# Both score matmuls of an attention kernel contract over all 128 partitions: each key band holds one part, high or low, on both halves of the partitions

## The chip, the cores and the metric

The kernel runs on one core of one Trainium2 chip. The metric is the device time of one execution in microseconds (us), from the first to the last instruction of the core, as the median of repeated runs.

## The reference

One layer of a streaming encoder: a normalised input is projected by one large weight matrix, a pooling mixer and a windowed attention run side by side, both are gated, and an output projection is added to the input. Cut to what matters here:

```python
def _gqa_sink_attend(q, k, v, mask, sinks):
    s = jnp.einsum('bcqhgd,bckhd->bchgqk', q, k) * (HEAD_DIM ** -0.5)
    s = jnp.where(mask[None, :, None, None, None, :], s, NEG_INF)
    sink = jnp.broadcast_to(sinks[None, None, :, :, None, None], s.shape[:-1] + (1,))
    p = jax.nn.softmax(jnp.concatenate([s, sink], axis=-1), axis=-1)[..., :-1]
    return jnp.einsum('bchgqk,bckhd->bcqhgd', p, v)

def reference(x, ...):            # h = [16 meta tokens; 1024 frames], D_MODEL = 2048
    hn = _rmsnorm(h, norm_g)
    proj = hn @ w_in
    pv, pg, q, k, v, ag = jnp.split(proj, SPLITS, axis=-1)
    pool_out = _multiscale_pool(pv, pool_w, pool_scale)
    attn_out = _attention_branch(q, k, v, q_norm_g, k_norm_g, sinks)
    mixed = jnp.concatenate([silu(pg) * pool_out, silu(ag) * attn_out], axis=-1)
    h = h + mixed @ w_out
```

There are 16 query heads and 2 key heads of dimension 64. The frames are cut into chunks of 64. The queries of a chunk see the 16 meta tokens, the previous chunk and their own chunk: 16 + 64 + 64 = 144 keys.

## The kernel before

**Precision.** Every matrix product is made of parts. A float32 number is split into a high part (rounded to the narrow matmul type, fp32r, by a copy on ScalarE, ACT) and a low part (the float32 number minus the high part, by a subtraction on VectorE, DVE). A projection is three matmuls: weight high by activation high, weight high by activation low, weight low by activation high (lines 1058, 1059 and 1062).

**Tiling and staging.** The 1024 frames are handled in two halves of 512 (`h` = 0, 1). In each half TensorE (PE) first projects keys and values (8 weight blocks of 128x512), then the 8 pairs of query heads (32 blocks), then 4 groups (`g`) of 24 blocks each, and then the output projection. Weight blocks come by DMA into `raw` (4 slots), ACT makes `wh`, DVE makes `wl`. ACT and DVE prepare the block three steps ahead of the one that TensorE works on, and ACT waits for a slot until TensorE has finished the block that was in it (`s_blk`).

**Key bands.** While the queries are projected, `k_band` on ACT (step 18) and on DVE (step 21) lays out the keys: for each key head `e` a band with 9 pieces of 64 + 16 columns, the 64 keys of a chunk and the 16 meta keys. `band_h` and `band_x` are both 128 partitions high. Before, `band_h` holds the high part on partitions 0 to 63 (its other half is not used), and `band_x` holds the low part on partitions 0 to 63 and the high part on 64 to 127. ACT counts its copies on `s_kbh`, DVE's last subtraction counts on `s_kbl`.

**Attention inside the groups.** A group has four units (`u` = 0 to 3), each of four chunks and two heads. A unit is worked between the blocks of the group: the scores after block 4u+3, the transposes of the probabilities after block 4u+8, the product with the values after block 4u+10. The order is written out by hand on each engine (`when` on TensorE, `todo` on ACT and DVE). The stationary operand of the scores, `qs[:, c]`, holds the high part of the queries on partitions 0 to 63 and the low part on 64 to 127. Per chunk there are two score matmuls of 144 columns into the PSUM tile `S`: line 1180 takes 64 partitions (query high by key high), line 1181 takes all 128 (query high by key low, plus query low by key high). In the first half the first chunk gets a third matmul that adds the mask, line 1184, which runs as two passes.

Four units by four groups by two halves are 32 units, with 8 score matmuls each: 256 in all. Eight of the 32 units have the mask.

**Around the scores on DVE.** `row_max` (line 890, output `smax`) waits for the last score matmul of the unit (`s_s`). `silu` (its reciprocal is line 948) follows in the same step of the list for `u` = 0 and 1. `p_low` (outputs `pt` and `pm`) waits for ACT's copies of the transposed probabilities, and the values matmuls (lines 1206 and 1210) wait for `p_low`.

**Around the bands on DVE.** After `k_band` come the low part of a weight block, `q_norm` (a reciprocal, line 842, and a product, line 844), another weight block and `square_low` (output named `d_l`, whose memory it uses), for which the sum of squares on TensorE (lines 1145 and 1146) waits.

Of the kernel before, what the change touches and what calls it, by code (L numbers as in the profile page):

```python
# [16 lines left out]
P = 128  # L17
D = 2048
KT = D // P
META = 16  # L20
# [9 lines left out]
CHUNK = 64  # L30
NCH = HALF // CHUNK
HD = 64
# [4 lines left out]
BAND = META + CHUNK  # L37
# [41 lines left out]
def hymba_layer(nc, xcat, norm_g, w_in, w_out, pool_w, vecs, consts, out):  # L79
# [6 lines left out]
    with ctx:  # L86
        def sb(name, shape, dt=f32):
            return ctx.enter_context(nc.sbuf_tensor(name, shape, dt))
# [11 lines left out]
        kT = sb("kT", [P, CHUNK + HALF])  # L100
        vT = sb("vT", [P, CHUNK + HALF])
        k_meta = sb("k_meta", [P, META])
# [13 lines left out]
        band_h = sb("band_h", [P, KVH, (NCH + 1) * BAND], f32r)  # L116
        band_x = sb("band_x", [P, KVH, (NCH + 1) * BAND], f32r)
# [310 lines left out]
        def _(act):  # L428
            def copy(dst, src):
                return nc.scalar.activation(dst, src, ACT.Copy)  # L430
# [55 lines left out]
            for h in range(HALVES):  # L486
# [36 lines left out]
                def k_band():  # L523
                    act.wait_ge(s_kn, SPANS_BY[h + 1])
                    for e in range(KVH):
                        src = slice(e * HD, (e + 1) * HD)
                        for band, dst in ((band_h, slice(0, HD)), (band_x, slice(HD, P))):
                            kb = band[dst, e, :].rearrange("p (c n) -> p c n", n=BAND)
                            copy(kb[:, :, 0:CHUNK],
                                 kT[src, :].rearrange("p (c n) -> p c n", n=CHUNK)).then_inc(s_kbh, 1)  # L530
                            copy(kb[:, :, CHUNK:BAND],
                                 k_meta[src, :].unsqueeze(1).to_broadcast([HD, NCH + 1, META])).then_inc(s_kbh, 1)
# [21 lines left out]
                for s in range(Q_BLKS + 1):  # L554
                    if s and s % 4 == 0:
                        q_square(s // 4 - 1)
                    if s < Q_BLKS:
                        split_high(h4 + KV_BLKS // RAW, s + LEAD)
                    if s > 4 and s % 4 == 1:
                        q_sqrt(s // 4 - 1)  # L560
                    if s == 2:
                        v_all_out()
                    if s == 18:
                        k_band()
                    if s == 23:
                        v_operand(0)
# [156 lines left out]
        def _(dve):  # L723
            def sub(dst, a, b):
                return nc.vector.tensor_tensor(dst, a, b, ALU.subtract)  # L725
# [63 lines left out]
            for h in range(HALVES):  # L789
# [26 lines left out]
                def k_band():  # L816
                    for e in range(KVH):
                        src = slice(e * HD, (e + 1) * HD)

                        high = (band_h, band_x)[e][src, e, :].rearrange("p (c n) -> p c n", n=BAND)  # L820
                        low = band_x[0:HD, e, :].rearrange("p (c n) -> p c n", n=BAND)
                        dve.wait_ge(s_kbh, 8 * h + (2, 8)[e])
                        sub(low[:, :, 0:CHUNK], kT[src, :].rearrange("p (c n) -> p c n", n=CHUNK),
                            high[:, :, 0:CHUNK])
                        ins = sub(low[:, :, CHUNK:BAND],
                                  k_meta[src, :].unsqueeze(1).to_broadcast([HD, NCH + 1, META]),
                                  high[:, :, CHUNK:BAND])
                    ins.then_inc(s_kbl, 1)

                def v_operand(e):  # L830
# [16 lines left out]
                for s in range(Q_BLKS + 1):  # L847
                    if s and s % 4 == 0:
                        square_low(s // 4 - 1)
                    if s < Q_BLKS:  # L850
                        split_low(h4 + KV_BLKS // RAW, s + LEAD)
                    if s > 4 and s % 4 == 2:
                        q_norm(s // 4 - 1)
                    if s == 21:
                        k_band()
                    if s == 25:
                        v_operand(0)
# [186 lines left out]
        def _(pe):  # L1044
            mm = nc.tensor.matmul
# [61 lines left out]
            for h in range(HALVES):  # L1107
# [58 lines left out]
                def group(g, e, late):  # L1166
                    G = h * GROUPS + g

                    def scores(u):
                        pe.wait_ge(s_qdl, G * UNITS + u + 1)  # L1170
                        pe.wait_ge(s_ex, ONE + (G * UNITS + u) * (QUAD + 1))
                        pe.wait_ge(s_kbh, 8 * (h + 1))
                        pe.wait_ge(s_kbl, ONE + h + 1)
                        for c in range(QUAD):
                            ch = (u % 2) * QUAD + c
                            o = S[:, c // 2, (c % 2) * KEYS:(c % 2 + 1) * KEYS]
                            at = slice(ch * BAND, ch * BAND + KEYS)
                            q = qs[:, c, :, :].rearrange("p a t -> p (a t)")
                            masked = h == 0 and ch == 0
                            mm(o, q[0:HD], band_h[0:HD, e, at], start=True, stop=False)  # L1180
                            last = mm(o, q, band_x[:, e, at], start=False, stop=not masked)  # L1181
                            if masked:

                                last = mm(o, ident, cst[:, C_MASK:C_MASK + KEYS],
                                          start=False, stop=True)
                        last.then_inc(s_s, 1)
# [29 lines left out]
                    for u in range(UNITS):  # L1216
                        when.setdefault(4 * u + 3, []).append((scores, u))
                        when.setdefault(4 * u + 8, []).append((transposes, u))
                        when.setdefault(4 * u + 10, []).append((values, u))
# [142 lines left out]
```

## Time and profile before

| | |
|---|---|
| median of 3 runs | 1302.7 us (1301.02, 1302.71, 1302.70) |
| span of the profiled execution | 1300.8 us |
| own time of the profiled execution | not recorded apart from its span |
| TensorE matmul busy | 1279.3 us, 98% |
| weight load busy | 1057.4 us, 81% |
| DVE busy | 895.0 us, 69% |
| ACT busy | 634.8 us, 49% |
| DMA | 103 GB/s over the span |
| granted TensorE clock | full in all 40 slices |

The busy time of TensorE counts matmuls whose ends are modelled and overlap the next one; how fast it gets on is read from the distances between the starts. The weight load (PEld) is listed apart from the matmul (PE) that uses it. A wait shown for an engine is the time that it stood idle before an instruction and who released it.

### The profile page before, as it was taken

The numbers are of one execution on the slowest core, as the hardware profiler recorded it, in microseconds if no ns is written. First come the engines' busy times: TensorE is split into PE (matmuls) and PEld (weight loads), VectorE is DVE, ScalarE is ACT, GpSimd is POOL, SyncE is SP. The second block draws the span as 40 slices with busy tenths as digits, with TensorE's granted clock in tenths as the row PEclk, the third lists the DMA queues.
The fourth block names the chain that finished last, engine by engine and source line by source line (L and its number), as shares of the span: only waits on it lengthen the run. The fifth ranks groups of instructions, "written<-read, shape, count | busy, mean of one in ns | idle before, by whom it ended". The sixth has DMA issues, their size and how long they took to land.

```text
span 1300.8 us, 19299 instructions
## 1 busy us (share of the span) xinstructions
PE 1279.3 (98%) x6200; PEld 1057.4 (81%) x6200; DVE 895.0 (69%) x1417; ACT 634.8 (49%) x1490; POOL 66.5 (5%) x78
## 2 busy tenths in 40 slices
PE   4999999999999999999999999999999999999998
PEld 4988798798888987888888887787887877788887
DVE  7466777878868777665644677777787887854553
ACT  6434356365454554545433344554645545444442
POOL 0000000010010110000000000000101103000000
PEclk9999999999999999999999999999999999999999
DMA  5233322322322225544543332223222222244442
GB/s 213 79 92 97 90 72 75 89 68 63 94 81 75 67 73 185 188 133 157 186 127 89 92 98 86 70 73 88 83 72 79 84 81 74 93 141 137 161 140 86
DMA packets 70609, 134.38 MB, mean 103 GB/s; under 512 B 8064, under 2 KB 10240, under 8 KB 69888
## 3 DMA queue, kind: packets, MB, share of 16 engines
q1 hardware_dynamic: 68160, 125.17, 31.4%
q0 software_dynamic: 2384, 8.39, 1.8%
q8 instruction: 35, 0.57, 0.2%
q14 instruction: 30, 0.25, 0.1%
HBM read 125.14 MB, written 8.39 MB: 103 GB/s over the span
## 4 chain that ended last, share of the span: by engine, by line
PE 94%; DVE 3%; DMA 1%; ACT 1%; issue 1%; SPq 0%; ACTq 0%
PE R L1058 18%; PE R L1059 18%; PE R L1062 18%; PE S L1281 4%; PE S L1282 4%; PE S L1280 4%; PE S L1181 3%; PE S L1180 3%; PE OP L1282 2%; PE OP L1280 2%; PE R L1281 2%; PE OP L1281 2%; PE R L1282 2%; PE R L1280 2%; PE OP L1059 1%; PE OP L1062 1%
## 5 line engine op out<-in xcount | busy, mean ns | idle before, releaser
L430 ACT ACTIVATE wh<-raw 128x512 fp32r<-128x512 f32 x400 | 250.3, 631 | 534.7 <-PE R L1062 310.1
L725 DVE TENSOR_TENSOR wl<-raw,wh 128x512 fp32r<-128x512 f32 x400 | 281.7, 708 | 264.7 <-ACT wh L430 263.6
L1058 PE MATMUL R<-act_h,wh 128*128 128x512 f32 (+1 forms) x1168 | 426.0, 370 | 0.0
L1059 PE MATMUL R<-act_l,wh 128*128 128x512 f32 (+1 forms) x1168 | 422.8, 367 | 0.0
L1062 PE MATMUL R<-act_h,wl 128*128 128x512 f32 (+1 forms) x1168 | 403.5, 366 | 0.0
L1058 PEld LDWEIGHTS R<-act_h,wh 128*128 128x128 f32 x1168 | 220.1, 188 | 36.4 <-DVE wl L725 0.8
L1059 PEld LDWEIGHTS R<-act_l,wh 128*128 128x128 f32 x1168 | 220.1, 188 | 34.7
L1062 PEld LDWEIGHTS R<-act_h,wl 128*128 128x128 f32 x1168 | 210.6, 188 | 36.7
L948 DVE RECIPROCAL scr<-scr 128x512 f32<-128x512 f32 x32 | 107.3, 3353 | 1.1
L402 POOL TENSOR_TENSOR scr<-scr 128x527 f32<-128x527 f32 (+3 forms) x40 | 48.7, 1217 | 837.6 <-ACT pv_last L430 378.2
L430 ACT ACTIVATE pm<-OP 16x128 fp32r<-16x128 f32 x256 | 68.1, 266 | 5.4
L842 DVE RECIPROCAL scr<-scr 128x512 f32<-128x512 f32 x16 | 53.5, 3346 | 4.3 <-ACT scr L551 4.3
L725 DVE TENSOR_TENSOR pt<-PT,pt 128x512 fp32r<-128x512 f32 x32 | 22.1, 691 | 46.9 <-ACT pm L430 46.9
L1282 PE MATMUL S<-wh,band_x 128*128 128x512 f32 x128 | 50.7, 396 | 0.0
L1281 PE MATMUL S<-wl,band_h 128*128 128x512 f32 x128 | 50.6, 395 | 0.0
L1280 PE MATMUL S<-wh,band_h 128*128 128x512 f32 x128 | 50.3, 393 | 0.0
L1280 PE MATMUL S<-wh,v_s 128*128 128x512 f32 x128 | 49.9, 390 | 0.0
L1282 PE MATMUL S<-wh,mix_x 128*128 128x512 f32 x128 | 49.9, 390 | 0.0
L1281 PE MATMUL S<-wl,v_s 128*128 128x512 f32 x128 | 49.8, 389 | 0.0
L610 ACT ACTIVATE scr<-S,nmax 128x144 f32<-128x144 f32 x128 | 46.8, 378 | 0.6
L725 DVE TENSOR_TENSOR mix_x<-mixed,v_s 128x512 fp32r<-128x512 f32 x64 | 43.8, 684 | 0.0
L725 DVE TENSOR_TENSOR band_x<-mixed,band_h 128x512 fp32r<-128x512 f32 x64 | 43.7, 683 | 0.0
(210 smaller groups left out, 1844.5 us busy)
## 6 DMA issues: line engine op xcount, KB each, us to landing
raw<-w_in_blocks SPq DMA_DIRECT2D x272, 256.0 KB, 2.6
raw<-w_out_in SPq DMA_DIRECT2D x128, 256.0 KB, 3.0
scr<-xcat SPq DMA_DIRECT2D x32, 256.0 KB, 4.4
mixed<-xcat SPq DMA_DIRECT2D x4, 1024.0 KB, 7.7
res<-xcat SPq DMA_DIRECT2D x16, 256.0 KB, 3.2
out<-scr POOLq DMA_DIRECT2D x14, 256.0 KB, 2.6
out<-res POOLq DMA_DIRECT2D x14, 256.0 KB, 4.2
scr<-pool_w_in SPq DMA_DIRECT2D x8, 256.0 KB, 3.0
```

What stands on the lines that cost most here:

```text
L402: ins = pool.tensor_tensor(dst[:, lo:COLS], src[:, lo:COLS], src[:, lo - step:COLS - step], ALU.add)
L430: return nc.scalar.activation(dst, src, ACT.Copy)
L610: nc.scalar.activation(prob[:, c, :], S[:, c // 2, (c % 2) * KEYS:(c % 2 + 1) * KEYS], ACT.Exp, bias=nmax[:, c:c + 1], accum_out=den[:, c: ...
L725: return nc.vector.tensor_tensor(dst, a, b, ALU.subtract)
L842: nc.vector.reciprocal(q_rs[t % 2], q_rs[t % 2]).then_inc(s_qrs, 1)
L948: nc.vector.reciprocal(gate[n], gate[n]).then_inc(s_gr, 1)
L1058: mm(o, wh[:, b, w], act_h[:, k, c], start=(k == 0), stop=False)
L1059: mm(o, wh[:, b, w], act_l[:, k, c], start=False, stop=False)
L1062: last = mm(o, wl[:, b, w], act_h[:, k, c], start=False, stop=(k == KT - 1))
L1280: mm(YB[r], mh, wh[:, k % SPLIT, :], start=(k == 0), stop=False)
L1281: mm(YB[r], mh, wl[:, k % SPLIT, :], start=False, stop=False)
L1282: last = mm(YB[r], ml, wh[:, k % SPLIT, :], start=False, stop=(k == KT - 1))
```

## The change

The copies on ACT write the high part of the keys to both halves of the partitions of `band_h`, where two of them went to `band_x` before. The subtractions on DVE write the low part to both halves of `band_x`, so that there are eight of them in a half of the frames where there were four. The first score matmul takes all 128 partitions of `qs` and `band_h`: (query high + query low) by key high. The second takes `band_x` as before, and gives (query high + query low) by key low, with a product of the two low parts that was not computed before.

```diff
@@ ACT k_band
-                        for band, dst in ((band_h, slice(0, HD)), (band_x, slice(HD, P))):
+                        for band, dst in ((band_h, slice(0, HD)), (band_h, slice(HD, P))):
@@ DVE k_band
-                        high = (band_h, band_x)[e][src, e, :].rearrange("p (c n) -> p c n", n=BAND)
-                        low = band_x[0:HD, e, :].rearrange("p (c n) -> p c n", n=BAND)
+                        high = band_h[src, e, :].rearrange("p (c n) -> p c n", n=BAND)
                         dve.wait_ge(s_kbh, 8 * h + (2, 8)[e])
-                        sub(low[:, :, 0:CHUNK], kT[src, :].rearrange("p (c n) -> p c n", n=CHUNK),
-                            high[:, :, 0:CHUNK])
-                        ins = sub(low[:, :, CHUNK:BAND],
-                                  k_meta[src, :].unsqueeze(1).to_broadcast([HD, NCH + 1, META]),
-                                  high[:, :, CHUNK:BAND])
+                        for dst in (slice(0, HD), slice(HD, P)):
+                            low = band_x[dst, e, :].rearrange("p (c n) -> p c n", n=BAND)
+                            sub(low[:, :, 0:CHUNK], kT[src, :].rearrange("p (c n) -> p c n", n=CHUNK),
+                                high[:, :, 0:CHUNK])
+                            ins = sub(low[:, :, CHUNK:BAND],
+                                      k_meta[src, :].unsqueeze(1).to_broadcast([HD, NCH + 1, META]),
+                                      high[:, :, CHUNK:BAND])
                     ins.then_inc(s_kbl, 1)
@@ PE scores
-                            mm(o, q[0:HD], band_h[0:HD, e, at], start=True, stop=False)
+                            mm(o, q, band_h[:, e, at], start=True, stop=False)
                             last = mm(o, q, band_x[:, e, at], start=False, stop=not masked)
```

On DVE, at step 21 of the query projection of the first half, the kernel before has these instructions between two weight blocks and in front of the next query normalisation:

```order
L725 TENSOR_TENSOR band_x<-kT,band_h 64x9x64
L725 TENSOR_TENSOR band_x<-k_meta,band_h 64x9x16
L725 TENSOR_TENSOR band_x<-kT,band_x 64x9x64
L725 TENSOR_TENSOR band_x<-k_meta,band_x 64x9x16
L725 TENSOR_TENSOR wl<-raw,wh 128x512
```

After the change the same place on DVE reads:

```order
L725 TENSOR_TENSOR band_x<-kT,band_h 64x9x64
L725 TENSOR_TENSOR band_x<-k_meta,band_h 64x9x16
L725 TENSOR_TENSOR band_x<-kT,band_h 64x9x64
L725 TENSOR_TENSOR band_x<-k_meta,band_h 64x9x16
L725 TENSOR_TENSOR band_x<-kT,band_h 64x9x64
L725 TENSOR_TENSOR band_x<-k_meta,band_h 64x9x16
L725 TENSOR_TENSOR band_x<-kT,band_h 64x9x64
L725 TENSOR_TENSOR band_x<-k_meta,band_h 64x9x16
L725 TENSOR_TENSOR wl<-raw,wh 128x512
```

Two pairs of subtractions more stand ahead of the weight block `wl`; the same happens in the second half. On ACT and on TensorE the number and the order of the instructions stay; only the operands differ.

## Rows read from the trace of the kernel before

**Rows 1.** Part 1 of the page: busy time, share, instructions.

```profile
PE 1279.3 (98%) x6200; PEld 1057.4 (81%) x6200; DVE 895.0 (69%) x1417; ACT 634.8 (49%) x1490; POOL 66.5 (5%) x78
```

**Rows 2.** The page's chain that ended last, by engine.

```profile
PE 94%; DVE 3%; DMA 1%; ACT 1%; issue 1%; SPq 0%; ACTq 0%
```

**Rows 3.** Waits of TensorE from 150 to 490 us: total, times, longest.

```profile
PE OP L1280 <- DVE mixed L940: 0.4, 1, 0.4
```

**Rows 4.** Line 1180: duration min/median/max in ns, first and last start.

```profile
L1180 PE MATMUL S<-band_h,qs x128: 329/331/336, 157.4 to 1092.4; 64*128 64x144 f32 x128
```

**Rows 5.** Timeline of TensorE's matmuls, an unmasked unit: start, duration.

```profile
170.44 0.40 PE L1059 MATMUL R<-act_l,wh 128*128 128x512 f32 x1
170.68 0.39 PE L1062 MATMUL R<-act_h,wl 128*128 128x512 f32 x1
171.00 0.33 PE L1180 MATMUL S<-band_h,qs 64*128 64x144 f32 x1
171.26 0.33 PE L1181 MATMUL S<-band_x,qs 128*128 128x144 f32 x1
...
173.01 0.33 PE L1058 MATMUL R<-act_h,wh 128*128 128x264 f32 x1
```

**Rows 6.** Timeline of the weight loads of the same unit.

```profile
170.45 0.19 PEld L1062 LDWEIGHTS R<-act_h,wl 128*128 128x128 f32 x1
171.00 0.18 PEld L1180 LDWEIGHTS S<-band_h,qs 64*128 64x128 f32 x1 [0.36 <-issue]
...
172.84 0.19 PEld L1181 LDWEIGHTS S<-band_x,qs 128*128 128x128 f32 x1
172.94 0.19 PEld L1058 LDWEIGHTS R<-act_h,wh 128*128 128x128 f32 x1
```

**Rows 7.** Timeline of TensorE around a unit with the mask.

```profile
157.13 0.39 PE L1062 MATMUL R<-act_h,wl 128*128 128x512 f32 x1
...
159.75 0.44 PE L1058 MATMUL R<-act_h,wh 128*128 128x512 f32 x1
```

**Rows 8.** Timeline of TensorE, transposes of 128 columns.

```profile
175.98 0.60 PE L1195 MATMUL PT<-cst,scr 128*128 128x128 f32 x4
176.42 0.27 PE L1197 MATMUL OP<-cst,pnm 128*128 128x128 f32 x1
```

**Rows 9.** Timeline of TensorE, values matmuls of 256 columns.

```profile
182.40 0.65 PE L1206 MATMUL OP<-pt,v_s 128*128 128x256 f32 x4
182.88 0.40 PE L1210 MATMUL OP<-pm,vm 96*128 96x256 f32 x2
```

**Rows 10.** Timeline of DVE around the second unit, second half.

```profile
896.21 0.69 DVE L725 TENSOR_TENSOR wl<-raw,wh 128x512 fp32r<-128x512 f32 x1 [2.02 <-ACT wh L430]
897.65 0.76 DVE L890 TENSOR_REDUCE smax<-S 128x4 f32<-128x576 f32 x1 [0.75 <-PE S L1181]
...
903.87 0.69 DVE L725 TENSOR_TENSOR pt<-PT,pt 128x512 fp32r<-128x512 f32 x1 [0.15 <-ACT pm L430]
904.58 1.19 DVE L725 TENSOR_TENSOR pm<-OP,pm 16x128 fp32r<-16x128 f32 x4
```

**Rows 11.** Timeline of the weight loads, first of the values after it.

```profile
906.18 0.65 PEld L1206 LDWEIGHTS OP<-pt,v_s 128*128 128x128 f32 x4
```

**Rows 12.** Timeline of DVE at the key bands, first half.

```profile
114.99 0.74 DVE L725 TENSOR_TENSOR band_x<-kT,band_h 64x576 fp32r<-64x576 f32 x1
...
115.97 0.75 DVE L725 TENSOR_TENSOR band_x<-kT,band_x 64x576 fp32r<-64x576 f32 x1
...
117.65 0.69 DVE L725 TENSOR_TENSOR wl<-raw,wh 128x512 fp32r<-128x512 f32 x1 [0.70 <-ACT wh L430]
...
123.61 0.69 DVE L725 TENSOR_TENSOR d_l<-scr,d_h 128x512 fp32r<-128x512 f32 x1 [0.61 <-ACT d_h L546]
```

**Rows 13.** Timeline of the weight loads, the next sum of squares.

```profile
124.84 0.19 PEld L1145 LDWEIGHTS OP<-d_h,pw_h 128*128 128x128 f32 x1
```

**Rows 14.** One group of the second half: busy time of each engine.

```profile
883.00:967.00 84.00, 84.00 (x381) 67.14 (x380) 65.62 (x116) 45.07 (x127) 4.83 (x4) 1.00 0.28 81
```

## The prediction

> **What bounds the kernel now.** I read the page's busy table first: TensorE's matmuls cover 98% of the span, DVE 69%, ACT 49% [rows 1]. Matmul ends are modelled, so this alone proves little. The chain that ended last comes next: 94% of it is TensorE [rows 2]. The waits settle it. Between 150 and 490 us, four whole groups of attention, TensorE waited for another engine only 0.4 us [rows 3]. So what shortens TensorE's own stream of matmuls in the groups shortens the kernel, until some other engine comes late. The remaining question is how fast TensorE moves, and for that durations (331 ns for a score matmul, [rows 4]) are of no use, since neighbours overlap. I read starts.
>
> In the projections two 512-column matmuls start 0.24 us apart (170.44, 170.68), and the load for the second begins at 170.45, 0.23 us ahead of its matmul, under the one before [rows 5, 6]. I use 0.23. At the scores this picture breaks. The load of the first score matmul starts at 171.00, together with its matmul, and the load unit stood idle for 0.36 us before it for no cause but "issue" [rows 5, 6]. The next score matmul starts at 171.26: 0.26 us for 144 columns, more than 512 columns take. Nothing is preloaded there.
>
> Is it the small width or the change of shape (64 rows, 128 rows, 64 rows ...)? The last pair of rows in the loads tells. After the last score matmul (128 rows) comes a projection matmul (128 rows): its load starts 0.10 us after the score's load (172.84, 172.94), and the matmul itself 0.17 us after (173.01) [rows 5, 6]. So 144 columns are no obstacle to preloading; the change between 64 and 128 rows is. The idle stretch at the entry into 64 rows says the same.
>
> The Trainium skill has this too: TensorEngine Tiling (Array Packing), Key Properties, says that changing the tiling mode drains TensorE. The trace agrees, with 0.26 us at each step.
>
> **The matmuls: what the change removes.** After it all eight score matmuls have 128 rows, as have their neighbours on both sides. The count stays. The price of a 144-column matmul of 128 rows among its like is not in the trace, so I bound it.
> - Below: the load to load distance of 0.10 us above [rows 6].
> - Near: five matmuls of 128 columns (four transposes and one more) start 0.44 us / 4 = 0.11 us apart (175.98 to 176.42) [rows 8].
> - Above: the values matmuls, 256 columns, 0.48 / 4 = 0.12 us (182.40 to 182.88) [rows 9].
> - Lowest of all: if only the columns counted. 512 columns take 0.23 and 256 take 0.12, a slope of 0.43 ns a column, which gives 0.07 us for 144. The transposes, at 0.11 with fewer columns, speak against it.
>
> I take 0.11, since 144 is nearest to 128.
>
> An unmasked unit takes 173.01 - 170.68 = 2.33 us from the last projection matmul before it to the first after it [rows 5]. After: 0.23 + 8 x 0.11 = 1.11. Saved: 1.22 us, in 24 units: 29.3 us. A unit with the mask takes 159.75 - 157.13 = 2.62 us [rows 7]. After: 0.23 + (8 + 2 passes) x 0.11 = 1.33. Saved: 1.29 us, in 8 units: 10.3 us. Together **39.6 us**. At 0.10 the 24 x 8 + 8 x 10 = 272 starts save 2.7 more, at 0.12 2.7 less; at 0.07 they save 10.9 more.
>
> **A rule that speaks against this.** The Trainium skill, TensorE: Matmul & The Clock Gate, Part 3 on packing small matmuls, says that a weight load overlaps a running matmul only when the row group differs. By it loads between 128-row matmuls would never hide, this change would have nothing to win, and the time would stay at 1302.7. The trace disagrees: the load at 170.45 runs under the matmul at 170.44, both of 128 rows [rows 5, 6].
>
> **DVE at the key bands: what the change adds.** Two more pairs of subtractions per half. A pair takes 115.97 - 114.99 = 0.98 us [rows 12], so 1.96 us. Behind them on DVE wait a weight block, the query normalisation and `square_low`. DVE idled 0.70 us before that weight block (117.65) and 0.61 us before `square_low` (123.61) [rows 12]; both pauses absorb it, leaving 1.96 - 0.70 - 0.61 = 0.65 us. `square_low` then ends at 123.61 + 0.69 + 0.65 = 124.95, and TensorE's load that waits for it began at 124.84 [rows 13]. That is 0.1 us late, with the signal's way some 0.15. Twice: **0.3 us**. Below: nothing. Above, were no pause there: 2 x 1.96 = 3.9 us. ACT makes as many copies of the same size as before, to another tile: nothing.
>
> **DVE in the groups: what comes late next.** TensorE gets faster by 1.2 us per unit while the others keep their work. Where does that catch up? `row_max` of the second unit waited 0.75 us for the last score matmul [rows 10]; the scores now end 1.2 us earlier, but DVE is free only after its weight block, at 896.21 + 0.69 = 896.90. So `row_max` starts 0.75 us earlier instead of 1.2: against TensorE's stream DVE has lost 0.45 us. It had 0.15 us of slack before `pt` (903.87), so `p_low` runs 0.3 us late; it ended at 904.58 + 1.19 = 905.77 and the load that waits for it stood at 906.18 [rows 10, 11], 0.41 us of slack. It is just enough; I put **0.3 us** for all groups together. No other wait spans the scores with so little room: the transposes follow the scores by five blocks, and ACT then starts its work on them anew, released by TensorE itself. In the rest of a group no score matmul runs, and distances stay. DMA has room, at 0.28 of its engines in such a group [rows 14].
>
> **Sum.** 39.6 - 0.3 - 0.3 = 39.0 us. Span: 1300.8 - 39.0 = 1261.8. The profiled execution's span lies 1.9 us under the median of the runs, 1302.7; I keep that distance: **1263.7 us**.
>
> **Rivals.**
> - *DVE takes over in part of the groups.* In a group of the second half DVE is busy 65.62 of 84 us [rows 14]; with 4.9 us less that is 65.62 / 79.1 = 83%, and averages hide bursts such as the reciprocals. If the 0.45 us that DVE loses at a unit came through in all 32 units, 14.4 us would be given back: 1278. For it: `p_low` is close. Against: before almost every unit DVE still waits for something of TensorE's or ACT's (2.02 us before 896.21). Chance 9%, between 1269 and 1285.
> - *Columns alone set the pace*, 0.07 us: 1263.7 - 10.9 = 1252.8. Against it stand the transposes. Chance 5%. The Trainium skill, TensorE: Matmul & The Clock Gate, Back-to-back issue gap, gives about 81 ns a matmul at 128 columns with loads in between; by it the sum would be 272 x 0.029 = 7.9 us lower than mine, an estimate. The rows show 0.11.
> - *The drain is not from the rows*, but belongs to the scores (their operand, the switch of bank): 0.26 stays, and 1302.7 with it, within a microsecond. The load at 172.94 speaks against it. Chance 6%, no measurable change.
> - *Slower.* The same, and the added subtractions reach TensorE in full, having lost their cover of 0.70 and 0.61 us: 1302.7 + 3.9 = 1306.6. It decides only if the matmuls win less than 1.3 us of those 3.9 back, and at least two thirds of the 1.96 us come through at each half. Chance 2%.
>
> **How the numbers follow.** Forecast 78%, its own range 1260 (0.10 us a start, no late DVE) to 1269 (0.12, and DVE late by 2 to 3 us). The range given reaches a part of the way to the two rivals on either side: 1256 to 1271. What is within 0.2% (2.6 us) could not be told from no change by measurement of this kernel. Faster 0.92, same 0.06, slower 0.02.
>
> **What the profile after would show.** Score matmuls 0.11 us apart, with each load started ahead of its matmul and no "issue" idle of 0.36 us at the first of a unit; 173.01 - 170.68 shrunk from 2.33 to about 1.1. `row_max` no longer waits for the second unit's scores. At the bands eight subtractions, and a wait of at most 0.2 us before the next sum of squares. The share of DVE up to about 71%. Wrong would make me: a score distance of 0.12 or more, or a new wait of TensorE for `wl` or `pm` in every group.

## The result and the profile after

The changed kernel takes 1262.79 us (median of 4 runs, 1261.46 to 1263.45); the kernel before takes 1302.59 us on the same chip (4 runs). The ratio is 0.9694, 95% interval 0.9683 to 0.9706: 39.8 us less. The forecast was 1263.7 us. The profiled execution's span is 1261.8 us, the number that the forecast gave for it; its own time, 1263.45 us, is the longest of the four, and the other three have spans of 1259.8, 1261.0 and 1261.2 us.

The page of the changed kernel, part 1 (busy time, share, instructions), against [rows 1]:

```profile
PE 1239.5 (98%) x6200; PEld 1042.5 (83%) x6200; DVE 896.2 (71%) x1425; ACT 635.4 (50%) x1490; POOL 68.6 (5%) x78
```

TensorE has the same 6200 matmuls and 39.8 us less of busy time. It is still 98% of its span: it was the bound and still is. DVE has 8 instructions and 1.2 us more. The chain by engine reads as before, 94% TensorE [rows 2].

The timeline of TensorE around the same unmasked unit as in [rows 5], changed kernel:

```profile
170.05 0.39 PE L1063 MATMUL R<-act_h,wl 128*128 128x512 f32 x1
170.28 0.23 PE L1181 MATMUL S<-band_h,qs 128*128 128x144 f32 x1
170.35 0.27 PE L1182 MATMUL S<-band_x,qs 128*128 128x144 f32 x1
170.46 0.27 PE L1181 MATMUL S<-band_h,qs 128*128 128x144 f32 x1
...
171.12 0.33 PE L1059 MATMUL R<-act_h,wh 128*128 128x264 f32 x1
```

The timeline of the weight loads there, against [rows 6]:

```profile
170.05 0.19 PEld L1181 LDWEIGHTS S<-band_h,qs 128*128 128x128 f32 x1
170.28 0.19 PEld L1182 LDWEIGHTS S<-band_x,qs 128*128 128x128 f32 x1
170.39 0.19 PEld L1181 LDWEIGHTS S<-band_h,qs 128*128 128x128 f32 x1
```

The first score load now starts at 170.05, together with the projection matmul ahead of it and 0.23 us before its own matmul at 170.28. Before, the load unit stood idle for 0.36 us, and the load then started together with its matmul. From the projection matmul ahead of the unit to the one behind it are 171.12 - 170.05 = 1.07 us, where there were 2.33 [rows 5]. The later score matmuls start 0.11 us apart. The unit with the mask, against [rows 7]:

```profile
157.77 0.39 PE L1063 MATMUL R<-act_h,wl 128*128 128x512 f32 x1
...
159.09 0.44 PE L1059 MATMUL R<-act_h,wh 128*128 128x512 f32 x1
```

That is 1.32 us, where there were 2.62. If all units were like these two, the matmuls would save 24 x 1.26 + 8 x 1.30 = 40.6 us. Measured in the same way from the starts of all 32 units in both traces, the 24 without a mask went from 56.0 to 26.6 us and the 8 with one from 21.0 to 10.6: together 39.8 us, which is the difference of the medians.

Four units are longer than the others, the third of each group in the second half: 1.23, 1.23, 1.27 and 1.27 us instead of 1.07 to 1.09, some 0.7 us in all. Behind their scores the program makes TensorE wait (`s_pve`) until ACT has finished `pv_out`, whose last instruction is the copy of `pv_last`. ACT and the weight loads in the changed kernel:

```profile
883.42 0.21 ACT L430 ACTIVATE scr<-pv_last 128x16 f32 x1
```
```profile
883.40 0.19 PEld L1182 LDWEIGHTS S<-band_x,qs 128*128 128x128 f32 x1
883.70 0.19 PEld L1059 LDWEIGHTS R<-act_h,wh 128*128 128x128 f32 x1
```

The same place in the kernel before:

```profile
910.59 0.21 ACT L430 ACTIVATE scr<-pv_last 128x16 f32 x1
```
```profile
911.94 0.19 PEld L1058 LDWEIGHTS R<-act_h,wh 128*128 128x128 f32 x1
```

Before, ACT's copy ended at 910.80, 1.14 us ahead of the load. Now it ends at 883.63, and the load comes at 883.70, 0.30 us behind the last score load instead of 0.11. The long scores had hidden `pv_out`. That this wait is the cause is read from the program and from these rows; no run tests it.

The waits of the loads in the changed kernel (total, times, longest) show where TensorE's loads wait for DVE. The changed kernel has one line more above these places, so L1206 of the kernel before is L1207 here:

```profile
PEld OP L1207 <- DVE pm L725: 0.5, 2, 0.2
...
PEld OP L1146 <- DVE d_l L725: 0.3, 2, 0.2
```

The last row is new: in each half the load waits 0.15 us before the sum of squares that comes behind the bands. No wait for `pm` was added. The matmul of that load does not come late, though:

```profile
125.51 0.39 PE L1063 MATMUL R<-act_h,wl 128*128 128x512 f32 x1
125.74 0.39 PE L1146 MATMUL OP<-d_h,pw_h 128*128 128x512 f32 x1
```
```profile
125.62 0.19 PEld L1146 LDWEIGHTS OP<-d_h,pw_h 128*128 128x128 f32 x1 [0.15 <-DVE d_l L725]
```

It starts 0.23 us behind its neighbour, the usual distance. The load is 0.12 us ahead of it instead of 0.23: its lead took up the delay. In the second half it is the same (746.63 to 746.86, load at 746.74).

### The profile page after: what moved, and what is told of

The parts are those of the page before. It is cut to its first block, busy times and chain, and to the rows that moved or that the text cites. A ratio compares the mean times of both kernels' runs of the same rounds, so it can differ in the third digit from the quotient of the medians.

```text
span 1261.8 us, 19307 instructions
## 1 busy us (share of the span) xinstructions
PE 1239.5 (98%) x6200; PEld 1042.5 (83%) x6200; DVE 896.2 (71%) x1425; ACT 635.4 (50%) x1490; POOL 68.6 (5%) x78
## 4 chain that ended last, share of the span: by engine, by line
PE 94%; DVE 3%; DMA 1%; ACT 1%; issue 1%; SPq 0%; ACTq 0%
PE R L1059 19%; PE R L1060 18%; PE R L1063 18%; PE S L1282 4%; PE S L1283 4%; PE S L1281 4%; PE OP L1283 2%; PE OP L1281 2%; PE R L1282 2%; PE OP L1282 2%; PE R L1283 2%; PE R L1281 2%; PE OP L1060 1%; PE OP L1063 1%; PE OP L1059 1%; PE OP L1207 1%
```

## The experiments

Eight experiments and a repeat of the changed kernel, each timed against the kernel before on the same chip. The first group asks what the 0.26 us belonged to.

**The bands alone.** The bands of the changed kernel, the first score matmul of the kernel before:

```diff
-                            mm(o, q, band_h[:, e, at], start=True, stop=False)
+                            mm(o, q[0:HD], band_h[0:HD, e, at], start=True, stop=False)
```

> The bands as in the changed kernel (high part on both halves, low part on both halves, eight subtractions), but the first score matmul takes 64 partitions as before. It leaves out query low by key high. My theory (the gain is the change of shape between 64 and 128 rows, the bands cost 0.3 us): 1302.6 + 0.3 = 1302.9 us, score matmuls 0.26 us apart. Rival (the added subtractions reach TensorE in full): 1302.6 + 3.9 = 1306.5. Rival (something in the layout of the bands gives the gain): about 1263.

Measured: 1302.37 us (before: 1302.56), ratio 0.9998, interval 0.9989 to 1.0008. Its timeline shows the old pace:

```profile
169.19 0.39 PE L1063 MATMUL R<-act_h,wl 128*128 128x512 f32 x1
169.51 0.33 PE L1181 MATMUL S<-band_h,qs 64*128 64x144 f32 x1
169.77 0.33 PE L1182 MATMUL S<-band_x,qs 128*128 128x144 f32 x1
...
171.52 0.33 PE L1059 MATMUL R<-act_h,wh 128*128 128x264 f32 x1
```

The data in the bands give nothing, and eight added subtractions (four in each half) cost less than the measurement can tell; here too the load of the sum of squares waits 0.15 us, and its matmul stands 0.23 us behind the one ahead (123.36, 123.59). The whole gain hangs on the number of partitions in the first score matmul. The rivals at 1306.5 and at 1263 fall.

**Half of the changes of shape.** The kernel before, with the two parts of every other chunk in the other order:

```diff
-                            mm(o, q[0:HD], band_h[0:HD, e, at], start=True, stop=False)
-                            last = mm(o, q, band_x[:, e, at], start=False, stop=not masked)
+                            parts = [(q[0:HD], band_h[0:HD, e, at]), (q, band_x[:, e, at])]
+                            if c % 2 == 0:
+                                parts.reverse()
+                            mm(o, *parts[0], start=True, stop=False)
+                            last = mm(o, *parts[1], start=False, stop=not masked)
```

> The kernel before with the same eight score matmuls of a unit in another order: 128 rows, 64 rows, 64, 128, 128, 64, 64, 128. Instead of 8 changes of shape an unmasked unit has 4 (a masked one 6, since the mask has 128 rows). If each change costs (2.33 - 1.11) / 8 = 0.153 us: 24 x 4 x 0.153 + 8 x 2 x 0.153 = 17.1 us saved, 1285.5 us; 64-row neighbours and 128-row neighbours 0.11 us apart. Rival (each 64-row matmul costs, wherever it stands): no gain, 1302.6.

Measured: 1283.21 us, ratio 0.9853, interval 0.9836 to 0.9869. Every matmul is one of the kernel before, with the same operands, and 19.4 us are gone, 2.3 more than expected; the 32 units by themselves save 18.4. TensorE's timeline:

```profile
169.70 0.39 PE L1062 MATMUL R<-act_h,wl 128*128 128x512 f32 x1
...
170.08 0.33 PE L1184 MATMUL S<-band_h,qs 64*128 64x144 f32 x1
...
171.38 0.33 PE L1058 MATMUL R<-act_h,wh 128*128 128x264 f32 x1
```

Before the load of the matmul at 170.08 the load unit is again idle for "issue":

```profile
169.70 0.19 PEld L1183 LDWEIGHTS S<-band_x,qs 128*128 128x128 f32 x1
170.08 0.18 PEld L1184 LDWEIGHTS S<-band_h,qs 64*128 64x128 f32 x1 [0.19 <-issue]
170.19 0.19 PEld L1183 LDWEIGHTS S<-band_h,qs 64*128 64x128 f32 x1
170.46 0.19 PEld L1184 LDWEIGHTS S<-band_x,qs 128*128 128x128 f32 x1
170.57 0.19 PEld L1183 LDWEIGHTS S<-band_x,qs 128*128 128x128 f32 x1
170.83 0.18 PEld L1184 LDWEIGHTS S<-band_h,qs 64*128 64x128 f32 x1
```

Loads of the same shape follow each other after 0.11 us (170.08, 170.19; 170.46, 170.57). A load of another shape comes after 0.27 us from 64 to 128 rows (170.19 to 170.46) and after 0.26 from 128 to 64 (170.57 to 170.83). It is not the 64-row matmul that costs, but the change, in both directions.

**96 rows.** The changed kernel with three quarters of the partitions in the first matmul:

```diff
-                            mm(o, q, band_h[:, e, at], start=True, stop=False)
+                            mm(o, q[0:96], band_h[0:96, e, at], start=True, stop=False)
```

> The changed kernel with 96 partitions in the first score matmul; part of query low by key high is left out. My theory (what drains is the change between the 64-row shape and the full one, and 96 rows count as the full one, as the values matmuls of 96 rows show): 1262.8 us, as the changed kernel. Rival (any change in the number of rows drains): 0.26 us a score matmul, 1302.6.

Measured: 1262.54 us, ratio 0.9693, interval 0.9677 to 0.9709, the time of the changed kernel. The rows give the shape as 96*128, and it runs beside 128*128 without a pause:

```profile
168.49 0.39 PE L1063 MATMUL R<-act_h,wl 128*128 128x512 f32 x1
168.72 0.23 PE L1181 MATMUL S<-band_h,qs 96*128 96x144 f32 x1
168.79 0.28 PE L1182 MATMUL S<-band_x,qs 128*128 128x144 f32 x1
168.90 0.28 PE L1181 MATMUL S<-band_h,qs 96*128 96x144 f32 x1
```

So a mere difference in rows costs nothing; the change between 64 rows and the full shape does. Row counts between 64 and 96 were not run. "Drain" is the name that the prediction and the expectations give to the pause; the rows show the pause and the late load, not what goes on in it.

**Both with 64 rows.** The kernel before, with the second matmul cut down as well:

```diff
-                            last = mm(o, q, band_x[:, e, at], start=False, stop=not masked)
+                            last = mm(o, q[0:HD], band_x[0:HD, e, at], start=False, stop=not masked)
```

> The kernel before with 64 partitions in both score matmuls; query low by key high is left out. A unit has 2 changes of shape (a masked one 4). If a change costs 0.153 us and 64-row matmuls run 0.11 us apart: 24 x 6 x 0.153 + 8 x 4 x 0.153 = 26.9 us saved, 1275.7 us. Rival (loads of 64-row matmuls never run ahead): 0.26 us stays, 1302.6. Second rival (they load in half the time and run 0.07 us apart): 10 us less than mine, 1266.

Measured: 1276.46 us, ratio 0.9799, interval 0.9783 to 0.9816. TensorE's timeline:

```profile
170.20 0.39 PE L1062 MATMUL R<-act_h,wl 128*128 128x512 f32 x1
170.52 0.33 PE L1180 MATMUL S<-band_h,qs 64*128 64x144 f32 x1
170.69 0.27 PE L1181 MATMUL S<-band_x,qs 64*128 64x144 f32 x1
...
171.57 0.39 PE L1058 MATMUL R<-act_h,wh 128*128 128x264 f32 x1
171.79 0.28 PE L1059 MATMUL R<-act_l,wh 128*128 128x264 f32 x1
```

Its second score load:

```profile
170.63 0.19 PEld L1181 LDWEIGHTS S<-band_x,qs 64*128 64x128 f32 x1
```

From the second one on the matmuls run 0.11 us apart, as those of 128 rows do, and the load at 170.63 runs ahead of its matmul at 170.69; only entry and exit cost. Both rivals fall. The four kernels make a line:

| kernel | changes of shape in an unmasked unit | length of the unit, us |
|---|---|---|
| before | 8 | 2.33 |
| half of the changes | 4 | 171.38 - 169.70 = 1.68 |
| both with 64 rows | 2 | 171.57 - 170.20 = 1.37 |
| changed | 0 | 1.07 |

A change costs 0.16, 0.16 and 0.15 us from line to line. The last figure is somewhat low: behind the unit of the 64-row kernel the projection matmuls start 0.22 us apart (171.57 to 171.79), where the other three have 0.17, so that each of its two changes costs nearer to 0.18.

**Half of the columns.** The question here is what sets the 0.11 us once the changes are gone. The run is the changed kernel with 72 columns instead of 144 (scores of half the keys are left out):

```diff
+                            n = KEYS if masked else KEYS // 2
+                            few = slice(ch * BAND, ch * BAND + n)
+                            part = o[:, 0:n]
-                            mm(o, q, band_h[:, e, at], start=True, stop=False)
-                            last = mm(o, q, band_x[:, e, at], start=False, stop=not masked)
+                            mm(part, q, band_h[:, e, few], start=True, stop=False)
+                            last = mm(part, q, band_x[:, e, few], start=False, stop=not masked)
```

> The changed kernel with only 72 of the 144 columns in both score matmuls (the eight masked chunks keep 144), so the scores of half the keys are left out. 248 matmuls are half as wide. My theory (after the change the pace of 0.11 us is that of the weight loads, whatever the columns): 1262.8 us and 0.11 us a matmul. Rival (the columns set the pace, at the slope of 0.43 ns each between 256 and 512 columns): 248 x 72 x 0.43 ns = 7.7 us less, 1255.

Measured: 1262.46 us, ratio 0.9692, interval 0.9679 to 0.9705. The loads keep their distance, and so do the matmuls but for one:

```profile
168.40 0.19 PEld L1184 LDWEIGHTS S<-band_h,qs 128*128 128x128 f32 x1
168.51 0.19 PEld L1185 LDWEIGHTS S<-band_x,qs 128*128 128x128 f32 x1
```
```profile
168.29 0.20 PE L1184 MATMUL S<-band_h,qs 128*128 128x72 f32 x1
168.32 0.27 PE L1185 MATMUL S<-band_x,qs 128*128 128x72 f32 x1
```

The second score matmul follows the first by 0.03 us, where it was 0.07 with 144 columns. That is lost again behind the unit, where the projection matmuls start 0.21 us apart instead of 0.17. Half of the columns saves nothing, so the columns do not set the pace of 0.11 us. What is left are the loads of 128 columns, 0.11 us apart; that they set it is argued, since no run has narrower loads.

The second group asks what the change costs on DVE, and was run together with the changed kernel.

> The changed kernel once more, on the chip of the three runs beside it, so that they can be compared with it to a few tenths of a microsecond. All theories: 1262.8 us, within 1.

Measured: 1262.87 us. The times below are compared with this one.

**More work at the bands.** The changed kernel, with two more subtractions for each key head:

```diff
+                        for half, dst in enumerate((slice(0, HD), slice(HD, P))):
+                            sub(mix_x[dst, e, :], kT[src, 0:BLK], band_h[src, e, 0:BLK])
                     ins.then_inc(s_kbl, 1)
```

> The changed kernel with four more subtractions of 64x512 behind the bands on DVE in each half, to a tile that nothing reads then; nothing of the result is changed. A subtraction takes 0.60 us from start to start, so 2.4 us a half. My theory (the cover of 1.3 us is used up by the change, so that all of it reaches the sum of squares on TensorE): a wait of 0.15 + 2.4 = 2.55 us in each half, 1262.8 + 4.8 = 1267.6. Rival (the sum of squares is covered elsewhere, or the time is caught up later in the half): under 1264.

Measured: 1269.90 us, 7.0 us more than the changed kernel; the ratios to the kernel before are 0.975 (0.9737 to 0.9763) and 0.9696 (0.9683 to 0.971). That is 2.3 us more than I expected. DVE's timeline at the bands and the load that waits:

```profile
117.12 1.38 DVE L725 TENSOR_TENSOR mix_x<-kT,band_h 64x512 fp32r<-64x512 f32 x2
118.52 0.75 DVE L725 TENSOR_TENSOR band_x<-kT,band_h 64x576 fp32r<-64x576 f32 x1
```
```profile
127.92 0.19 PEld L1148 LDWEIGHTS OP<-d_h,pw_h 128*128 128x128 f32 x1 [2.95 <-DVE d_l L725]
```

My estimate of the added work was short: a pair takes 118.52 - 117.12 = 1.40 us, so 2.8 us a half and not 2.4. The wait is 2.95 us, which is 0.15 + 2.8 to the hundredth. In the matmuls, too, it is 2.8 us: the one of the waiting load and the two behind it come 2.91 + 0.34 + 0.24 us apart instead of 3 x 0.23. The cover was used up exactly, and what comes on top reaches TensorE in full. The two halves wait 5.6 us more than the changed kernel. Of the remaining 1.4 us of the measured 7.0, about 1.0 stands in the two profiles before any band is laid out (the first sum of squares after 100 us starts at 102.03 here and at 101.02 in the repeat of the changed kernel), so it is not a cost of the subtractions. The two profiles of the changed kernel itself differ by 1.5 us there (102.53 and 101.02).

**Zeros instead of copies.** The bands of the kernel before with four subtractions, the upper half of `band_h` zeroed, and 128 rows (the second fill, for the second half, stands behind GpSimd's output loop):

```diff
+            pool.wait_ge(s_init, 5)
+            pool.memset(band_h[HD:P, :, :].bitcast(f32), 0.0).then_inc(s_init, 1)
...
+                        pe.wait_ge(s_init, 6 + h)
...
-                            mm(o, q[0:HD], band_h[0:HD, e, at], start=True, stop=False)
+                            mm(o, q, band_h[:, e, at], start=True, stop=False)
```

> The bands of the kernel before (four subtractions a half), the upper half of band_h filled with zeros by GpSimd before each half, and the first score matmul with 128 rows: the same products as in the kernel before, in the shape of the changed one. My theory: the whole gain of the shape, without the 0.3 us of the subtractions: 1262.8 - 0.3 = 1262.5, and no wait before the sum of squares behind the bands. Rival (the copies or the values in the bands matter): above 1264.

Measured: 1263.53 us, ratio 0.9698, interval 0.9685 to 0.9711: not to be told from the changed kernel, nor from the 0.3 us less that was expected. The wait before the sum of squares is gone, since DVE has its pauses back, 0.71 us before the weight block and 0.61 before `d_l`:

```profile
122.35 0.69 DVE L729 TENSOR_TENSOR d_l<-scr,d_h 128x512 fp32r<-128x512 f32 x1 [0.61 <-ACT d_h L550]
```

The sums are those of the kernel before; the 64 rows added to the first matmul multiply zeros. The gain is there whole, so only the shape counts. Neither this kernel nor that with 96 rows is measurably better than the changed one.

**More work for DVE in the groups.** The changed kernel, with this behind `row_max`:

```diff
+                        for i in range(2):
+                            sub(mix_x[:, i, :], kT[:, 0:BLK], kT[:, 0:BLK])
```

> The changed kernel with two more subtractions of 128x512 (0.60 us each) on DVE behind row_max in every unit, 32 x 1.2 = 38.4 us of DVE time that nothing reads; the result is the same. My theory (only the low parts behind the second unit are close: the values matmuls' load stood 0.22 us behind them in the second half and 0.75 us in the first): 4 x (1.2 - 0.22) + 4 x (1.2 - 0.75) = 5.7 us, 1268.5. Rival (DVE is the bound of the groups or close to it): up to all of it, 1301.

Measured: 1269.61 us, 6.7 us more than the changed kernel and 1.1 more than I expected, ratio to before 0.975 (0.9737 to 0.9763). Of 38 us of added work less than a fifth shows. The waits of the loads:

```profile
PEld OP L1209 <- DVE pm L725: 7.9, 12, 1.3
```

They are 7.4 us above the changed kernel's. One of them:

```profile
881.24 0.54 PEld L1209 LDWEIGHTS OP<-pt,v_s 128*128 128x128 f32 x4 [1.07 <-DVE pm L725]
```

Eight of the twelve are where I expected them, at the values of a group's first unit, 0.43 to 0.47 us in the first half and 1.07 to 1.29 in the second. Two of 0.5 us at later units of the last groups were not expected, and the remaining two stand in the changed kernel too. DVE is not the bound of the groups, but at one place in each of them it is close to it.

## Why the prediction was right, point by point

**What bounds the kernel.** TensorE was the bound and stayed so. A shortening of its own stream came through whole: 39.8 us in the 32 units, 39.8 in the medians.

**The reason of the 0.26 us.** The forecast read it from one pair of loads in the kernel before, 0.10 us apart where the shape stayed the same [rows 6]. The experiments bear it out from four sides: fewer changes with the same matmuls, 96 rows, 64 rows throughout, and the old arithmetic with zeros. The rival that the drain belongs to the scores falls with the reordered kernel.

**The price afterwards.** 0.11 us was taken from the transposes of 128 columns [rows 8]; it is what the rows show. The rival in which the columns alone set the pace falls with the 72-column kernel. Small misses: the second score matmul follows the first by 0.07 us, which makes a unit 1.07 us long and not 1.11; the masked one came out at 1.32 for 1.33. The sum of this term was 39.6 us and measured 39.8. Two misses stand against each other in it: 40.6 by the ordinary units, less the 0.7 us of the four that wait for `pv_out`.

**The rule that speaks against this** (the Trainium skill, TensorE: Matmul & The Clock Gate, Part 3: a weight load overlaps a running matmul only when the row group differs) is refuted for this use. In the kernel with 64 rows in both, the load at 170.63 runs under the 64-row matmul of 170.52 to 170.85, on the same rows, and in the changed kernel the load at 170.39 under the 128-row matmul at 170.35.

**DVE at the bands.** The wait was right and its price was not. 0.15 us a half was forecast for the load, and the load waits 0.15 us; with more work there, the wait grew by exactly that work. But the forecast took the delay of the load for one of TensorE's stream ("Twice: 0.3 us"). The load usually starts 0.23 us ahead of its matmul, and it came 0.11 us late without delaying it: the term is zero. That was all there was to give. With the added subtractions the load came 2.91 us late and the matmuls behind it 2.80.

**DVE in the groups.** This term was mis-sized: the forecast put 0.3 us for all groups together, and it measured zero. The mechanism is there. `row_max` of the second unit no longer waits for the scores, and the low parts run later, as DVE's timeline of the changed kernel shows (against [rows 10]):

```profile
870.32 0.69 DVE L725 TENSOR_TENSOR wl<-raw,wh 128x512 fp32r<-128x512 f32 x1 [1.80 <-ACT wh L430]
870.93 0.75 DVE L891 TENSOR_REDUCE smax<-S 128x4 f32<-128x576 f32 x1
...
876.30 0.68 DVE L725 TENSOR_TENSOR wl<-raw,wh 128x512 fp32r<-128x512 f32 x1
876.90 0.68 DVE L725 TENSOR_TENSOR pt<-PT,pt 128x512 fp32r<-128x512 f32 x1
877.60 1.19 DVE L725 TENSOR_TENSOR pm<-OP,pm 16x128 fp32r<-16x128 f32 x4
```
```profile
879.01 0.65 PEld L1207 LDWEIGHTS OP<-pt,v_s 128*128 128x128 f32 x4
```

They end at 877.60 + 1.19 = 878.79, 0.22 us ahead of the load, where the kernel before had 0.41. So 0.19 of the slack went, not 0.3, and the rest was enough. At `row_max` the loss is the 0.45 us of the forecast: from it to the load were 906.18 - 897.65 = 8.53 us [rows 10, 11], and now are 879.01 - 870.93 = 8.08. But from `row_max` to `pt` DVE caught up 0.25 us (6.22 to 5.97) and not 0.15. A DVE instruction begins a little before the one ahead of it is shown to end (876.30 + 0.68 = 876.98, next start 876.90), so an idle time of 0.15 us hides somewhat more room.

**A wait that the forecast did not see.** "No other wait spans the scores with so little room" does not hold. ACT's `pv_out` starts when the block ahead of the scores is done, and TensorE waits for its end behind them. In the second half it had 1.14 us of room, and the scores got 1.26 us shorter. That costs some 0.7 us in all, about as much as the 0.6 us that the forecast put down to DVE.

**That the sum hit the span to the tenth** is luck. The sum was 39.0 us and the medians moved 39.8, since both terms of 0.3 us were nothing. The profiled execution was the longest of its four, which made up for that: the changed kernel's second profile has a span of 1260.0 us, the first 1261.8. One execution's time lies 1.65 us above its own span (1263.45 and 1261.8); the 1.9 us of the forecast compared a median with the span of another execution.

## What to carry to other kernels

Read the distances between the starts of matmuls and of their weight loads, not durations: a load that starts together with its own matmul was not run ahead, and it is worth asking what the matmul before it had that was different. If a 64-row matmul stands among full ones, either give it the full rows (a copy or zeros in the unused half did equally well here), or order the matmuls so that equal shapes stand together; each change cost 0.16 us here, more than the 0.11 of a small matmul. Before relying on such a gain, list every wait of the engine right behind the shortened place, look for the one with the smallest slack, and count how much of it the change spends. A load that waits is a cost only where its matmul comes late too: look at the matmul's distance to the one ahead.

## What the runs show of the hardware

- A matmul of 96 rows counts as a full one, while one of 64 does not: no pause at 96 beside 128, 0.27 us between the loads at 64 beside 128.
- Beside loads of 128 columns, matmuls of 72 and of 144 columns cost the same, 0.11 us.
- The first of several small matmuls behind a long one is passed quickly: 0.07 us from it to the second (170.28 to 170.35) with 144 columns and 0.03 with 72, then 0.11 in both. The first two were expected before their runs; this one was not.
- A load that waited 0.15 us for DVE did not delay its matmul, which stood 0.23 us behind the one ahead as always.
